# One TensorE side group per head instead of two in a chunked recurrence, with eight level products packed into two banks

## The chip, the cores and the metric

The kernel runs on one core of one Trainium2 chip. The time is that of the device, in microseconds, for one execution of the whole program; the lower, the better. TensorE is written PE in the profile, its weight loads PEld, VectorE DVE, ScalarE ACT, GpSimd POOL and SyncE, which issues most of the DMAs, SP.

## What is computed

The reference is two model blocks on 512 tokens of width 2048, in float32. The first block normalises the input, multiplies it by a large `w_in`, and splits the product into a gated short convolution and a recurrent part; the second is an attention and retention block. Nearly all of the arithmetic is in dense products with weight matrices. What the change touches is the recurrent part, cut to its core here (8 heads, 128 features in each, log decays `log_f` that differ by feature):

```python
def step(state, inp):                      # one chunk of tokens, all heads
    qn, kn, vn, fn = inp
    b = jnp.cumsum(fn, axis=2)
    inter = jnp.einsum('bhtk,bhkv->bhtv', qn * jnp.exp(b), state)
    diff = b[:, :, :, None, :] - b[:, :, None, :, :]
    decay = jnp.exp(jnp.where(causal, diff, 0.0)) * causal_f
    a = jnp.einsum('bhtk,bhtsk,bhsk->bhts', qn, decay, kn)
    o = inter + jnp.einsum('bhts,bhsv->bhtv', a, vn)
    b_last = b[:, :, -1:, :]
    state = (jnp.exp(b_last[:, :, 0, :])[..., None] * state
             + jnp.einsum('bhsk,bhsv->bhkv', kn * jnp.exp(b_last - b), vn))
    return state, o
```

The matrix `a` has the decay inside its sum over the features, so it is no plain product of q and k.

## The kernel before

**Dense work.** Each weight matrix is read in units of 256 rows by 512 columns (`UNITS`), by SP into `RAW`. ScalarE rounds a unit to its high part (`WH`, line 395), VectorE subtracts to get the low part (`WL`, line 418), and TensorE makes three products for each (high by high, high by low, low by high) into four banks of PSUM, in `pe_dense` at line 366. A group of 512 columns takes 16 steps of k for a 2048-row matrix, 12 dense matmuls in each. `hi_upto` and `lo_upto` let the splits run two units ahead of TensorE.

**Side work.** Each engine's program is a generator. After each dense step, `Turns.after_step` lets one piece of the queue `specials` be written, up to its next bare `yield`, and one of `chores`. The recurrence of the eight heads is such side work: `hgrn_pe`, `hgrn_act`, `hgrn_dve`, `hgrn_sp`, one after the other, among the dense groups `cg`, `xa`, `bg`, `za` of each half (heads 0 to 3 in the first, 4 to 7 in the second). So the order is fixed when the program is written, and `idle(n)` leaves n steps without a side piece.

**One head.** The kernel computes `a` for chunks of 128 tokens by levels. Level 0 is the diagonal; level L pairs blocks of h = 2^(L-1) tokens with the block behind them, so that the decay can be put into q and k one level at a time. For each level ScalarE makes two exponentials (lines 895, 901), VectorE multiplies them into q and k (lines 1000 and 1004; the rows are those of `level_rows`), and then brings two running sums on (lines 1008, 1012). Levels 2 to 7 have only four rows of scratch, `XX[:, 0..2]` and `XX4`, and levels 5 and 6 use rows of levels 3 and 2 again: hence in `hgrn_dve`, for `lev > 4`, a wait for the products of levels 0 to 3.

TensorE makes all products of a head in tiles of 32 output rows (`tile_position=(0, y)`), in two side groups:

- the first, after `idle(3)`: levels 0 and 1 (line 782, 16 matmuls) into one bank, levels 2 and 3 (line 798, 32 matmuls) into the other;
- the second, four steps later: levels 4 and 5 (line 798, 32 matmuls), levels 6 and 7 (line 782, 8 and 8 matmuls).

Each of these float32 matmuls is two passes in the trace, so a group is 96 passes. Two of the eight banks (6 and 7) are for side work, and all side groups take them in turn. VectorE copies the products out of the banks into `AT` by `take_diagonal` (line 937), `take_pairs` (948), `take_within` (958) and `take_across` (974). After the two groups come the sums over a chunk (line 825, 6 passes) and the values (lines 857 and 860, 14 passes), both in whole 128-row form.

Of the kernel before, what the change touches and what calls it, by code (L numbers as in the profile page):

```python
# [224 lines left out]
def build(nc, xT, pT, vec, logits, cst, masks, ident, w_in, w_a, w_b, w_o, w_gate, w_proj,  # L225
# [528 lines left out]
    XX4 = sb("XX4", [512], F32, W0 + 98560)  # L754
    XQ = sb("XQ", [16, 48], F32, W0 + 98560)

    def level_rows(lev):
        return XX4[:, :] if lev == 7 else XX[:, {2: 2, 3: 1, 4: 0, 5: 1, 6: 2}[lev]]

    QUERIES = XX[:, 1]  # L760
# [6 lines left out]
    def hgrn_pe(i, hh):  # L767
        half = hh // 4
        kk, q = KK[:, i], Q[:, i]

        def product_bank(levels):
            b, was = special_bank(("prod", hh, levels[0]), dve, ("take", hh, levels[-1]))
            for lev in levels:
                banks["prod", hh, lev] = banks["prod", hh, levels[0]]
            if was:
                T.wait_ge(was[0], (yield was))
            return b

# [12 lines left out]
        def within_tiles(lev, b, at):  # L791
            h = 1 << (lev - 1)
            T.wait_ge(dve, (yield dve, ("xl", hh, lev)))
            for n in range(16):
                y = 32 * n % 128
                t = level_rows(lev)[:, 32 * n:32 * n + 32]
# [5 lines left out]
        def across_tiles(b):  # L802
            T.wait_ge(dve, (yield dve, ("xl", hh, 6)))
            x = level_rows(6)
            for n in range(8):
                c, p = n // 2, n % 2
                tile_product(b, 64 * p + 32 * (c % 2), 32 * (c // 2),
                             x[:, 64 * n:64 * n + 32], x[:, 64 * n + 32:64 * n + 64])

        def across_halves(b):  # L810
            T.wait_ge(dve, (yield dve, ("xl", hh, 7)))
            x = level_rows(7)
            for n in range(8):
                c, p = n // 2, n % 2
                ins = tile_product(b, 64 * (c % 2) + 32 * p, 64 + 64 * (c // 2),
                                   x[:, 64 * n - 32 * p:64 * n - 32 * p + 32], x[:, 128 * c + 64:128 * c + 128])
            return ins

        def chunk_sums(b):
            for j in range(4):  # L820
                T.wait_ge(ev_a, (yield ev_a, (("iv", half), j)))
            T.wait_ge(keys_turned, (yield keys_turned, hh))
            T.wait_ge(keys_turned2, (yield keys_turned2, hh))
            for c in range(3):
                ins = nc.tensor.matmul(b[:, CH[c]], KT[:, c], VN[:, c, 128 * i:128 * i + 128], start=True, stop=True)  # L825
            ins.then_inc(side.sem, side.step(("sums", hh)))

        yield from idle(3)
        b = yield from product_bank((0, 1))
        yield from pairs_and_diagonal(b)  # L830
        b = yield from product_bank((2, 3))
        yield from within_tiles(2, b, 0)
        ins = yield from within_tiles(3, b, 256)
        ins.then_inc(side.sem, side.step(("prod", hh, 3)))
        yield
        yield from idle(3)
        b = yield from product_bank((4, 5))
        yield from within_tiles(4, b, 0)
        yield from within_tiles(5, b, 256)
        b = yield from product_bank((6, 7))  # L840
# [80 lines left out]
    def hgrn_dve(i, hh):  # L921
        half = hh // 4
        lf, kk, q, r = LF[:, i], KK[:, i], Q[:, i], RR[:, :]

        def take_diagonal():
            b = bank[banks["prod", hh, 0]]
# [12 lines left out]

        def take_pairs():  # L940
            b = bank[banks["prod", hh, 0]]
            V.wait_ge(side, (yield side, ("prod", hh, 3)))
# [7 lines left out]

        def take_within(lev):
            h = 1 << (lev - 1)
            at = 256 if lev in (3, 5) else 0
            src = bank[banks["prod", hh, lev]][:, at:at + 256].rearrange("p (c n x) -> p c n x", c=4, x=h)
            msk = late(MASK[:, lev], lev).unsqueeze(1).broadcast_to([128, 4, 64 // h, h])
            V.wait_ge(side, (yield side, ("prod", hh, 3 if lev < 4 else 7)))
            V.wait_ge(dve, (yield dve, ("take", hh, lev - 1)))
            nc.vector.copy_predicated(ATD.rearrange("p c (n x) -> p c n x", x=2 * h)[:, :, :, h:], msk, src
                                      ).then_inc(dve.sem, dve.step(("take", hh, lev)))

        def take_across(lev):
            b = bank[banks["prod", hh, lev]]
            V.wait_ge(side, (yield side, ("prod", hh, 7)))
            V.wait_ge(dve, (yield dve, ("take", hh, lev - 1)))
            w = 32 * (lev - 5)
            for odd in range(2):
                for p in range(2):
                    if lev == 6:
                        y, rows, cols, at = 64 * p + 32 * odd, slice(64 * p, 64 * p + 32), 64 * p + 32, 0
                    else:  # L970
                        y, rows, cols, at = 64 * odd + 32 * p, slice(32 * p, 32 * p + 32), 64, 64
                    src = b[y:y + 32, at:at + 2 * w].rearrange("p (c t) -> p c t", c=2)
                    dst = ATD[rows, odd::2, cols:cols + w]
                    ins = nc.vector.tensor_copy(dst, src)
            ins.then_inc(dve.sem, dve.step(("take", hh, lev)))

        for lev in range(1, 8):
# [7 lines left out]
            V.wait_ge(act, (yield act, ("up", hh, lev)))  # L985
            V.wait_ge(ev_d, (yield ev_d, (("q", half), i)))
            if lev > 4:
                V.wait_ge(side, (yield side, ("prod", hh, 3)))
            elif hh % 4:
                V.wait_ge(dve, (yield dve, ("o", hh - 1)))  # L990
            if lev == 1:
# [4 lines left out]
                                        E[:, 1:512:2].rearrange("p (n x) -> p n x", x=16), ALU.mult  # L996
                                        ).then_inc(dve.sem, dve.step(("xu", hh, 1), ("xl", hh, 1)))
            else:
                X = level_rows(lev)
# [6 lines left out]
            if lev > 1:  # L1006
# [22 lines left out]
        if hh:  # L1029
# [5 lines left out]
        yield from take_within(4)  # L1035
        yield from take_within(5)
# [5 lines left out]
        yield from take_across(6)  # L1042
        yield
        yield from take_across(7)
        yield
        yield
# [1727 lines left out]
```

## Time and profile before

| | us |
|---|---|
| median of 3 runs | 2510.53 (2509.77 to 2511.0) |
| profiled execution | 2509.97 |
| its span, first to last instruction | 2508.7 |
| PE busy | 2502.2 (100%) |
| PEld busy | 2075.9 (83%) |
| DVE busy | 1358.9 (54%) |
| ACT busy | 918.4 (37%) |
| POOL busy | 149.5 (6%) |

The span is what the trace covers; the execution has 1.3 us around it. Busy time of PE is the union of its matmuls' modelled durations, which overlap: a dense matmul is shown as 0.39 us long, while the next one starts 0.23 us behind it. So the distance between starts, not the duration, is what a matmul costs. In a timeline row "x32" are instructions merged into one row, the first number is when the first of them starts, the second how long they last together, to the modelled end of the last.

### The profile page before, as it was taken

What the parts mean: (1) busy time and instruction counts of PE and PEld (TensorE: products, weight loads), DVE (VectorE), ACT (ScalarE), POOL (GpSimd) and SP (SyncE); (2) the same over time, 40 slices, a digit from 0 to 9 for tenths busy, and PEclk for the clock granted to TensorE, in tenths of its full rate; (3) what the DMA queues carried; (4) which work ended last, traced back from release to release, by engine and by line L of the source; (5) the groups of instructions that cost most, each with busy time, mean ns of one, the idle gap of its engine ahead of it and who ended that gap; (6) DMA issues with size and microseconds to landing.
All of it is one profiled execution on the core that took longest, in us unless ns stands there. A gap on an engine that the chain in (4) does not pass through costs nothing.

```text
span 2508.7 us, 31305 instructions
## 1 busy us (share of the span) xinstructions
PE 2502.2 (100%) x12614; PEld 2075.9 (83%) x12614; DVE 1358.9 (54%) x2248; ACT 918.4 (37%) x1259; POOL 149.5 (6%) x195
## 2 busy tenths in 40 slices
PE   9999999999999999999999999999999999999999
PEld 8888888888888888888888888888888888888888
DVE  7557744567544555655443363485256555665425
ACT  6633325333332222322232253443344344544423
POOL 0011110012100000000001103200000000000001
PEclk9999999999999999999999999999999999999999
DMA  5333333333335666666443232236222243433432
GB/s 192 110 96 95 96 105 95 95 95 100 100 93 164 213 218 214 218 212 212 149 161 110 93 101 93 93 101 178 92 76 76 85 125 101 113 106 112 178 101 101
DMA packets 213633, 317.95 MB, mean 127 GB/s; under 512 B 66736, under 2 KB 69680, under 8 KB 212464
## 3 DMA queue, kind: packets, MB, share of 16 engines
q1 hardware_dynamic: 208592, 312.55, 40.2%
q0 software_dynamic: 4320, 2.99, 0.5%
q8 instruction: 99, 1.62, 0.3%
q10 hardware_dynamic: 576, 0.42, 0.1%
q14 instruction: 46, 0.38, 0.1%
HBM read 295.43 MB, written 8.39 MB: 121 GB/s over the span
## 4 chain that ended last, share of the span: by engine, by line
PE 100%; ACT 0%; DVE 0%; issue 0%; ACTq 0%; DVEq 0%
PE bank L366 94%; PE bank L1449 1%; PE bank L1450 1%; PE bank L1451 1%; PE bank L798 0%; PE bank L857 0%; PE bank L782 0%; PE bank L860 0%; PE bank L825 0%; PE bank L1841 0%; PE bank L1955 0%; PE bank L1953 0%; PE bank L1954 0%; PE bank L467 0%; ACT OT L2266 0%; PE bank L472 0%
## 5 line engine op out<-in xcount | busy, mean ns | idle before, releaser
L366 PE MATMUL bank<-XH,WH 128*128 128x512 f32 (+1 forms) x2776 | 1078.7, 390 | 0.0
L366 PE MATMUL bank<-XH,WL 128*128 128x512 f32 (+1 forms) x2776 | 1074.5, 389 | 0.0
L366 PE MATMUL bank<-XL,WH 128*128 128x512 f32 (+1 forms) x2776 | 1074.0, 389 | 0.0
L418 DVE TENSOR_TENSOR WL<-RAW,WH 128x1024 fp32r<-128x1024 f32 x430 | 530.1, 1234 | 760.6 <-ACT WH L395 760.0
L395 ACT CAST WH<-RAW 128x1024 fp32r<-128x1024 f32 x430 | 450.1, 1048 | 1113.4 <-PE bank L366 1102.2
L366 PEld LDWEIGHTS bank<-XH,WL 128*128 128x128 f32 x2776 | 521.0, 188 | 108.1 <-DVE WL L418 0.2
L366 PEld LDWEIGHTS bank<-XH,WH 128*128 128x128 f32 x2776 | 521.0, 188 | 107.7 <-ACT WH L395 0.2
L366 PEld LDWEIGHTS bank<-XL,WH 128*128 128x128 f32 x2776 | 521.2, 188 | 107.1 <-issue 0.5
L366 PE MATMUL bank<-WH,XL 128*128 128x512 f32 x384 | 149.4, 389 | 0.0
L366 PE MATMUL bank<-WH,XH 128*128 128x512 f32 x384 | 149.4, 389 | 0.0
L366 PE MATMUL bank<-WL,XH 128*128 128x512 f32 x384 | 149.4, 389 | 0.0
L1234 DVE CUSTOM_DVE_ANT_0 AST<-AST,CB 128x512 f32<-128x512 f32 x192 | 125.1, 685 | 10.0 <-DMA AST<-in_w_ada 9.8
L366 PE MATMUL bank<-YH,WH 128*128 128x512 f32 x256 | 97.7, 389 | 0.0
L366 PE MATMUL bank<-YH,WL 128*128 128x512 f32 x256 | 97.6, 389 | 0.0
L366 PE MATMUL bank<-YL,WH 128*128 128x512 f32 x256 | 97.6, 389 | 0.0
L366 PEld LDWEIGHTS bank<-WH,XH 128*128 128x128 f32 x384 | 72.1, 188 | 15.1
L366 PEld LDWEIGHTS bank<-WL,XH 128*128 128x128 f32 x384 | 72.1, 188 | 14.9
L366 PEld LDWEIGHTS bank<-WH,XL 128*128 128x128 f32 x384 | 72.1, 188 | 14.9
L2597 POOL TENSOR_TENSOR AC<-AC,GT 128x512 f32<-128x512 f32 x15 | 22.7, 1512 | 748.0 <-ACT GT L2087 746.4
L366 PEld LDWEIGHTS bank<-YL,WH 128*128 128x128 f32 x256 | 48.0, 188 | 10.0
L366 PEld LDWEIGHTS bank<-YH,WL 128*128 128x128 f32 x256 | 48.0, 188 | 10.0
L366 PEld LDWEIGHTS bank<-YH,WH 128*128 128x128 f32 x256 | 48.1, 188 | 10.0
(351 smaller groups left out, 1882.7 us busy)
## 6 DMA issues: line engine op xcount, KB each, us to landing
RAW<-in_w_in SPq DMA_DIRECT2D x303, 512.0 KB, 3.8
AST<-in_w_ada SPq DMA_DIRECT2D x192, 256.0 KB, 4.1
RAW<-in_w_o SPq DMA_DIRECT2D x32, 512.0 KB, 3.7
RAW<-in_w_gate SPq DMA_DIRECT2D x32, 512.0 KB, 3.6
RAW<-in_w_out SPq DMA_DIRECT2D x32, 512.0 KB, 3.7
RAW<-in_w_a SPq DMA_DIRECT2D x16, 512.0 KB, 4.2
RAW<-in_w_b SPq DMA_DIRECT2D x16, 512.0 KB, 4.3
PT<-ZT SPq DMA_DIRECT2D x256, 32.0 KB, 1.9
```

Of the source, the lines that this page charges most:

```text
L366: ins = nc.tensor.matmul(bank[b][:, cols], l, r[:, cols], start=first, stop=final)
L395: nc.scalar.copy(high_of(m), RAW[:, m % NRAW]).then_inc(hi.sem, hi.step(m))
L418: nc.vector.tensor_tensor(low_of(m), RAW[:, m % NRAW], high_of(m).bitcast(F32), ALU.subtract).then_inc(lo.sem, lo.step(m))
L1234: nc.vector.tensor_tensor_reduce(AST[:, n % 3], AST[:, n % 3], CB[:, q % 2], 1.0, 0.0, ALU.mult, ALU.add, PART[:, n:n + 1]).then_inc(dve.s ...
L1449: nc.tensor.matmul(b, high, right_high, start=start, stop=False)
L1450: nc.tensor.matmul(b, high, right_low, start=False, stop=False)
L1451: return nc.tensor.matmul(b, low, right_high, start=False, stop=stop)
L2597: nc.gpsimd.tensor_tensor(AC[:, 0], AC[:, 0], GT[:, j % 4], ALU.add).then_inc(pool.sem, pool.step(("acc1", j)))
```

## The change

`JOINED = range(8)` names the heads that have one side group instead of two; it is all of them. What it does for a head:

- `level_rows` gives levels 5, 6 and 7 rows of their own, in buffers that are idle at that time: rows of `YA` for heads 0 to 3, of `O` for head 4, of `LF`, `KK` and `Q` for heads 5 to 7. The wait at `lev > 4` goes.
- `hgrn_pe` has `idle(7)` and then all eight levels at once, at the step where the second group was. Levels 0 to 3 go to one bank and 4 to 7 to the other. To fit, levels 3 and 5 are packed by the new `half_of_tiles`: 64 columns instead of 256. The number of matmuls stays.
- `hgrn_dve` takes no product at levels 5 and 6 any more. All takes stand behind the last level. Levels 3 and 5 are taken by the new `take_half_of_tiles`, in four pieces each instead of one.
- The event that tells VectorE of levels 0 to 3 is now that of level 7 (`early`).

```diff
-    def level_rows(lev):
+    JOINED = range(8)
+
+    def level_rows(hh, lev):
+        if hh in JOINED and lev > 4:
+            if hh < 4:
+                return YA[:, lev - 1]
+            return O[:, lev] if hh == 4 else (LF, KK, Q)[lev - 5][:, hh - 5]
         return XX4[:, :] if lev == 7 else XX[:, {2: 2, 3: 1, 4: 0, 5: 1, 6: 2}[lev]]
...
+        def half_of_tiles(lev, b, at):
+            h = 1 << (lev - 1)
+            T.wait_ge(dve, (yield dve, ("xl", hh, lev)))
+            for n in range(16):
+                y = 32 * (n % 4)
+                t = level_rows(hh, lev)[:, 32 * n:32 * n + 32]
+                c = slice(at + 16 * (n // 4), at + 16 * (n // 4) + 16)
+                nc.tensor.matmul(b[y:y + 32, c].rearrange("p (n x) -> p n x", x=h), t,
+                                 late(t, lev), start=True, stop=True, tile_position=(0, y))
...
-        yield from idle(3)
-        b = yield from product_bank((0, 1))
-        yield from pairs_and_diagonal(b)
-        b = yield from product_bank((2, 3))
-        yield from within_tiles(2, b, 0)
-        ins = yield from within_tiles(3, b, 256)
-        ins.then_inc(side.sem, side.step(("prod", hh, 3)))
-        yield
-        yield from idle(3)
-        b = yield from product_bank((4, 5))
-        yield from within_tiles(4, b, 0)
-        yield from within_tiles(5, b, 256)
-        b = yield from product_bank((6, 7))
-        yield from across_tiles(b)
-        ins = yield from across_halves(b)
+        if hh in JOINED:
+            yield from idle(7)
+            b = yield from product_bank((0, 1, 2, 3))
+            yield from pairs_and_diagonal(b)
+            yield from within_tiles(2, b, 192)
+            yield from half_of_tiles(3, b, 448)
+            b = yield from product_bank((4, 5, 6, 7))
+            yield from within_tiles(4, b, 0)
+            yield from half_of_tiles(5, b, 256)
+            yield from across_tiles(b, 320)
+            ins = yield from across_halves(b, 384)
...
+        def take_half_of_tiles(lev):
...
+            for y in range(0, 128, 32):
+                rows = slice(y, y + 32)
+                if lev == 5:
+                    ins = nc.vector.tensor_copy(ATD[y:y + 16, :, y + 16:y + 32],
+                                                b[y:y + 16, at:at + 64].rearrange("p (c x) -> p c x", c=4))
+                    continue
+                src = b[rows, at:at + 64].rearrange("p (c n x) -> p c n x", c=4, x=h)
+                msk = late(MASK[rows, lev, rows], lev).unsqueeze(1).broadcast_to([32, 4, 16 // h, h])
+                ins = nc.vector.copy_predicated(
+                    ATD[rows, :, rows].rearrange("p c (n x) -> p c n x", x=2 * h)[:, :, :, h:], msk, src)
...
             if lev > 4:
-                V.wait_ge(side, (yield side, ("prod", hh, 3)))
+                if hh not in JOINED:
+                    V.wait_ge(side, (yield side, ("prod", hh, 3)))
...
-            if lev == 5:
+            if lev == 5 and hh not in JOINED:
                 yield from take_diagonal()
                 yield from take_pairs()
-            if lev == 6:
+            if lev == 6 and hh not in JOINED:
                 yield from take_within(2)
                 yield from take_within(3)
...
+        if hh in JOINED:
+            yield from take_half_of_tiles(3)
+            yield from take_within(4)
+            yield
+            yield from take_half_of_tiles(5)
+            yield from take_across(6)
+            yield
+            yield from take_across(7)
+            yield
```

TensorE, the products of head 0, before; `XQ` and `XX` hold the levels' rows, and 48 dense matmuls (left out at "...") stand between the groups:

```order
L366 MATMUL bank<-XH,WL 128x512
L782 MATMUL bank<-XQ,KK 32x48 x16
L798 MATMUL bank<-XX 32x16 x32
L366 MATMUL bank<-XH,WH 128x512
...
L366 MATMUL bank<-XH,WL 128x512
L798 MATMUL bank<-XX 32x16 x32
L782 MATMUL bank<-XX 32x32 x8
L782 MATMUL bank<-XX_89 32x64 x8
L366 MATMUL bank<-XH,WH 128x512
```

And the same place in the changed kernel, where line 788 is the old 782, line 804 the old 798, and line 815 the new `half_of_tiles`:

```order
L366 MATMUL bank<-XH,WL 128x512
L788 MATMUL bank<-XQ,KK 32x48 x16
L804 MATMUL bank<-XX 32x16 x16
L815 MATMUL bank<-XX 32x16 x16
L804 MATMUL bank<-XX 32x16 x16
L815 MATMUL bank<-YA 32x16 x16
L788 MATMUL bank<-YA 32x32 x8
L788 MATMUL bank<-YA 32x64 x8
L366 MATMUL bank<-XH,WH 128x512
```

The 96 matmuls of a head are the same ones; 48 of them moved 48 dense matmuls down, to stand ahead of the other 48.

VectorE, head 0, before, from the last products of level 6 to the last take; `WL` is a dense split:

```order
L1012 TENSOR_TENSOR LF<-LF 128x8x32
L958 COPY_PREDICATED AT<-MASK,bank 128x128x2
L958 COPY_PREDICATED AT<-MASK,bank 128x64x4
...
L418 TENSOR_TENSOR WL<-RAW,WH 128x1024
L1027 TENSOR_TENSOR KEYS<-KK,EE 128x384
L1032 STREAM_TRANSPOSE ZK<-KEYS 128x384
L958 COPY_PREDICATED AT<-MASK,bank 128x32x8
L958 COPY_PREDICATED AT<-MASK,bank 128x16x16
L418 TENSOR_TENSOR WL<-RAW,WH 128x1024
L1040 TENSOR_TENSOR XX<-Q,EE 128x384
L974 COPY AT<-bank 32x2x32 x4
L974 COPY AT<-bank 32x2x64 x4
```

In the changed kernel from the same split on (line 1076 is the old 1027, 1081 the old 1032, 966 the old 937, 977 the old 948, 987 the old 958, 1022 the old 974; 999 and 1004 are the new takes of levels 5 and 3):

```order
L1076 TENSOR_TENSOR KEYS<-KK,EE 128x384
L1081 STREAM_TRANSPOSE ZK<-KEYS 128x384
L966 COPY_PREDICATED AT<-MASK,bank 32x4x32 x4
L977 COPY_PREDICATED AT<-MASK,bank 32x4x16 x4
L987 COPY_PREDICATED AT<-MASK,bank 128x128x2
L418 TENSOR_TENSOR WL<-RAW,WH 128x1024
L1094 TENSOR_TENSOR XX<-Q,EE 128x384
L1004 COPY_PREDICATED AT<-MASK,bank 32x4x4x4 x4
L987 COPY_PREDICATED AT<-MASK,bank 128x32x8
L999 COPY AT<-bank 16x4x16 x4
L1022 COPY AT<-bank 32x2x32 x4
L418 TENSOR_TENSOR WL<-RAW,WH 128x1024
```

The takes of levels 0 to 3 have left the levels' own steps and stand behind the keys; the splits keep their number and their order among the steps.

## Rows read from the trace of the kernel before

**Rows 1.** The page: TensorE's busy time, its instruction queue, the chain that ended last.
```profile
PE 2502.2 (100%) x12614; PEld 2075.9 (83%) x12614; DVE 1358.9 (54%) x2248; ACT 918.4 (37%) x1259; POOL 149.5 (6%) x195
...
q8 instruction: 99, 1.62, 0.3%
...
PE 100%; ACT 0%; DVE 0%; issue 0%; ACTq 0%; DVEq 0%
```

**Rows 2.** Timeline of PE (start, duration, instruction, count): first group of head 0.
```profile
148.06 0.39 PE L366 MATMUL bank<-XH,WL 128*128 128x512 f32 x1
148.37 0.55 PE L782 MATMUL bank<-XQ,KK 128*32 128x48 f32 x32
148.74 0.73 PE L798 MATMUL bank<-XX 128*32 128x16 f32 x64
149.40 0.50 PE L366 MATMUL bank<-XH,WH 128*128 128x512 f32 x1
149.74 0.39 PE L366 MATMUL bank<-XL,WH 128*128 128x512 f32 x1
...
152.04 0.39 PE L366 MATMUL bank<-XH,WL 128*128 128x512 f32 x1
```

**Rows 3.** Timeline of PE: second group of head 0, the dense matmuls around it.
```profile
160.20 0.39 PE L366 MATMUL bank<-XH,WL 128*128 128x512 f32 x1
160.52 0.70 PE L798 MATMUL bank<-XX 128*32 128x16 f32 x62
...
161.56 0.50 PE L366 MATMUL bank<-XH,WH 128*128 128x512 f32 x1
161.90 0.39 PE L366 MATMUL bank<-XL,WH 128*128 128x512 f32 x1
```

**Rows 4.** Timeline of PE: the 128-row sums of head 0.
```profile
172.36 0.39 PE L366 MATMUL bank<-XH,WL 128*128 128x512 f32 x1
...
173.48 0.40 PE L366 MATMUL bank<-XL,WH 128*128 128x512 f32 x1
```

**Rows 5.** Waits of PEld (line, releaser, us in total, times, longest).
```profile
PEld bank L782 <- issue: 2.8, 8, 0.4
PEld bank L798 <- issue: 2.1, 6, 0.4
...
PEld bank L366 <- DVE WL L418: 0.2, 1, 0.2
```

**Rows 6.** DMA queues (packets, MB, share of 16 engines), 210 to 215 us.
```profile
q8 instruction: 1, 0.02, 1.6%
```

**Rows 7.** Timeline of PE: start of the second group of head 2.
```profile
262.75 0.71 PE L798 MATMUL bank<-XX 128*32 128x16 f32 x62
```

**Rows 8.** Timeline of DVE: around that group.
```profile
255.39 1.23 DVE L948 COPY_PREDICATED AT<-MASK,bank 32x64 f32<-32x64 uint16 x4
...
260.04 1.21 DVE L958 COPY_PREDICATED AT<-MASK,bank 128x256 f32<-128x256 uint16 x2
...
261.49 0.42 DVE L1004 TENSOR_TENSOR XX<-KK,EE 128x256 f32<-128x256 f32 x1
...
266.95 0.90 DVE L958 COPY_PREDICATED AT<-MASK,bank 128x256 f32<-128x256 uint16 x2
...
269.35 2.13 DVE L974 COPY AT<-bank 32x64 f32<-32x64 f32 x8
```

**Rows 9.** Groups of DVE instructions by form (count, busy us, mean ns, idle before).
```profile
L948 DVE COPY_PREDICATED AT<-MASK,bank 32x64 f32<-32x64 uint16 x32 | 9.5, 298 | 0.6
L974 DVE COPY AT<-bank 32x64 f32<-32x64 f32 x32 | 7.0, 218 | 0.3
```

**Rows 10.** Windows (busy us by engine, then granted clock, DMA share, GB/s).
```profile
160.00:162.00 2.00, 2.00 (x101) 1.51 (x100) 1.97 (x4) 1.73 (x3) 0.53 (x1) 1.00 0.05 4
...
2502.00:2505.00 3.00, 1.57 (x15) 1.33 (x13) 2.47 (x9) 2.15 (x7) 0.00 (x0) 1.00 1.01 384
2505.00:2508.70 3.70, 0.00 (x0) 0.00 (x0) 0.39 (x1) 0.45 (x1) 0.00 (x0) 0.77 0.77 293
```

More of the change, by code:

```diff
@@ L800, in within_tiles, with across_tiles, across_halves @@
             return ins
-        def across_tiles(b):
+        def half_of_tiles(lev, b, at):
[3 more added lines that the diff above has]
+                y = 32 * (n % 4)
+                t = level_rows(hh, lev)[:, 32 * n:32 * n + 32]
+                c = slice(at + 16 * (n // 4), at + 16 * (n // 4) + 16)
+                nc.tensor.matmul(b[y:y + 32, c].rearrange("p (n x) -> p n x", x=h), t,
+                                 late(t, lev), start=True, stop=True, tile_position=(0, y))
+        def across_tiles(b, at):
             T.wait_ge(dve, (yield dve, ("xl", hh, 6)))
-            x = level_rows(6)
+            x = level_rows(hh, 6)
             for n in range(8):
                 c, p = n // 2, n % 2
-                tile_product(b, 64 * p + 32 * (c % 2), 32 * (c // 2),
+                tile_product(b, 64 * p + 32 * (c % 2), at + 32 * (c // 2),
                              x[:, 64 * n:64 * n + 32], x[:, 64 * n + 32:64 * n + 64])
-        def across_halves(b):
+        def across_halves(b, at):
             T.wait_ge(dve, (yield dve, ("xl", hh, 7)))
-            x = level_rows(7)
+            x = level_rows(hh, 7)
             for n in range(8):
                 c, p = n // 2, n % 2
-                ins = tile_product(b, 64 * (c % 2) + 32 * p, 64 + 64 * (c // 2),
+                ins = tile_product(b, 64 * (c % 2) + 32 * p, at + 64 * (c // 2),
                                    x[:, 64 * n - 32 * p:64 * n - 32 * p + 32], x[:, 128 * c + 64:128 * c + 128])
@@ L826, in chunk_sums @@
             ins.then_inc(side.sem, side.step(("sums", hh)))
-        yield from idle(3)
-        b = yield from product_bank((0, 1))
-        yield from pairs_and_diagonal(b)
-        b = yield from product_bank((2, 3))
-        yield from within_tiles(2, b, 0)
-        ins = yield from within_tiles(3, b, 256)
-        ins.then_inc(side.sem, side.step(("prod", hh, 3)))
-        yield
-        yield from idle(3)
-        b = yield from product_bank((4, 5))
-        yield from within_tiles(4, b, 0)
-        yield from within_tiles(5, b, 256)
-        b = yield from product_bank((6, 7))
-        yield from across_tiles(b)
-        ins = yield from across_halves(b)
+        if hh in JOINED:
[9 more added lines that the diff above has]
+            ins = yield from across_halves(b, 384)
+        else:
+            yield from idle(3)
+            b = yield from product_bank((0, 1))
+            yield from pairs_and_diagonal(b)
+            b = yield from product_bank((2, 3))
+            yield from within_tiles(2, b, 0)
+            ins = yield from within_tiles(3, b, 256)
+            ins.then_inc(side.sem, side.step(("prod", hh, 3)))
+            yield
+            yield from idle(3)
+            b = yield from product_bank((4, 5))
+            yield from within_tiles(4, b, 0)
+            yield from within_tiles(5, b, 256)
+            b = yield from product_bank((6, 7))
+            yield from across_tiles(b, 0)
+            ins = yield from across_halves(b, 64)
         ins.then_inc(side.sem, side.step(("prod", hh, 7)))
@@ L923, in hgrn_dve @@
         lf, kk, q, r = LF[:, i], KK[:, i], Q[:, i], RR[:, :]
+        early = ("prod", hh, 7 if hh in JOINED else 3)
         def take_diagonal():
@@ L931, in take_diagonal @@
                 V.wait_ge(pool, (yield pool, "at0"))
-            V.wait_ge(side, (yield side, ("prod", hh, 3)))
+            V.wait_ge(side, (yield side, early))
             for y in range(0, 128, 32):
@@ L941, in take_pairs @@
             b = bank[banks["prod", hh, 0]]
-            V.wait_ge(side, (yield side, ("prod", hh, 3)))
+            V.wait_ge(side, (yield side, early))
             V.wait_ge(dve, (yield dve, ("take", hh, 0)))
@@ L952, in take_within @@
             h = 1 << (lev - 1)
-            at = 256 if lev in (3, 5) else 0
+            at = 256 if lev in (3, 5) else 192 if lev == 2 and hh in JOINED else 0
             src = bank[banks["prod", hh, lev]][:, at:at + 256].rearrange("p (c n x) -> p c n x", c=4, x=h)
             msk = late(MASK[:, lev], lev).unsqueeze(1).broadcast_to([128, 4, 64 // h, h])
-            V.wait_ge(side, (yield side, ("prod", hh, 3 if lev < 4 else 7)))
+            V.wait_ge(side, (yield side, early if lev < 4 else ("prod", hh, 7)))
             V.wait_ge(dve, (yield dve, ("take", hh, lev - 1)))
@@ L959, in take_within @@
                                       ).then_inc(dve.sem, dve.step(("take", hh, lev)))
+        def take_half_of_tiles(lev):
+            h = 1 << (lev - 1)
+            at = 448 if lev == 3 else 256
+            b = bank[banks["prod", hh, lev]]
+            V.wait_ge(side, (yield side, ("prod", hh, 7)))
+            V.wait_ge(dve, (yield dve, ("take", hh, lev - 1)))
+            for y in range(0, 128, 32):
[8 more added lines that the diff above has]
+                    ATD[rows, :, rows].rearrange("p c (n x) -> p c n x", x=2 * h)[:, :, :, h:], msk, src)
+            ins.then_inc(dve.sem, dve.step(("take", hh, lev)))
         def take_across(lev):
+            a6, a7 = (320, 384) if hh in JOINED else (0, 64)
             b = bank[banks["prod", hh, lev]]
@@ L968, in take_across @@
                     if lev == 6:
-                        y, rows, cols, at = 64 * p + 32 * odd, slice(64 * p, 64 * p + 32), 64 * p + 32, 0
+                        y, rows, cols, at = 64 * p + 32 * odd, slice(64 * p, 64 * p + 32), 64 * p + 32, a6
                     else:
-                        y, rows, cols, at = 64 * odd + 32 * p, slice(32 * p, 32 * p + 32), 64, 64
+                        y, rows, cols, at = 64 * odd + 32 * p, slice(32 * p, 32 * p + 32), 64, a7
                     src = b[y:y + 32, at:at + 2 * w].rearrange("p (c t) -> p c t", c=2)
@@ L998, in hgrn_dve @@
             else:
-                X = level_rows(lev)
+                X = level_rows(hh, lev)
                 nc.vector.tensor_tensor(vw(X)[:, :, h:], vw(q)[:, :, h:], vw(E)[:, :, h:], ALU.mult
@@ L1034, in hgrn_dve @@
         yield
-        yield from take_within(4)
-        yield from take_within(5)
+        if hh in JOINED:
+            yield from take_diagonal()
+            yield from take_pairs()
+            yield from take_within(2)
+        else:
+            yield from take_within(4)
+            yield from take_within(5)
         yield
@@ L1041, in hgrn_dve @@
                                 ).then_inc(dve.sem, dve.step(("queries", hh)))
[L1042 to L1046, printed above, removed]
+        if hh in JOINED:
+            yield from take_half_of_tiles(3)
+            yield from take_within(4)
+            yield
[3 more added lines that the diff above has]
+            yield from take_across(7)
+            yield
+        else:
+            yield from take_across(6)
+            yield
+            yield from take_across(7)
+            yield
+            yield
         V.wait_ge(side, (yield side, ("sums", hh)))
```

2 lines of the change are left out of this document (removed).

## The prediction

> **What bounds the kernel now.** I read the page first. TensorE is busy for 2502.2 of 2508.7 us, and the chain of what ended last is TensorE by 100% [rows 1]. So the time is the sum of the distances between TensorE's starts, and another engine counts only where it makes TensorE wait. The list of TensorE's waits shows none of that in the recurrent part: the one wait for a low part of weights in the whole program is 0.2 us, and what stands ahead of the side groups is "issue", 0.35 us each (2.8 us over 8 times), a cost of going over and not a wait for data [rows 5]. The view that decides is therefore the timeline of TensorE around the side groups.
>
> **What a group costs now.** Dense matmuls start every 0.2267 us: from 152.04 to 160.20 there are 36 steps, 8.16 us [rows 2, 3]. Around the first group of head 0 the last dense one starts at 148.06 and the twelfth one behind the group at 152.04 [rows 2]. Undisturbed, twelve steps are 12 x 0.2267 = 2.72 us; they took 3.98. The group costs 1.26 us. The same over two steps of the second group: 161.90 - 160.20 = 1.70, less 0.45, is 1.25; with the 0.02 to 0.03 us by which the next dense ones are a little slow (the first group has 1.68 - 0.45 = 1.23 over two steps, and 1.26 over twelve), 1.27.
>
> How much of that is the 96 passes, and how much is paid once for a group? The last pass starts 0.73 - 0.18 = 0.55 us behind 148.74 (a pass of this form is shown as 0.18 us long), at 149.29. So the passes themselves go from 148.37 to 149.29, 0.92 us, 9.6 ns each. The rest, 1.26 - 0.92 = 0.34 us, comes once: the first pass starts 0.31 us behind the last dense matmul instead of 0.23; the first dense one 0.11 us behind the last pass; the next one 0.34 us behind that instead of 0.23; and the slow steps after it. In the second group the same reading gives about 0.90 us of passes and 0.35 to 0.37 once.
>
> **The change, part by part.**
>
> *One group instead of two.* No matmul goes and none is added; 192 passes stand in one row, 0.92 + 0.90 us and one distance between them of 0.01. Once per head 0.34 us falls away. The distance between a 48-column pass and a 16-column one is already inside the first group, as that from 16 to 32 columns is in the second, and neither shows. Eight heads: 8 x 0.34 = 2.7 us. The bounds: no more can go than all that is paid once, 8 x 0.37 = 3.0 us. For the lower end I take the sums, six passes that keep the 128-row form: 173.48 - 172.36 = 1.12, less 0.45, is 0.67 us [rows 4], so that at a ninth to a tenth of a microsecond for each pass (128 of 512 columns would be a quarter of 0.2267, two passes and the weight loads make it more) hardly 0.1 us is paid once. If only that were saved, it is 0.8 us. The groups here change from 128 to 32 rows and back, and their own rows have the 0.34, so I take 2.7.
>
> *Packing of levels 3 and 5.* 16 matmuls of 16 columns each as before, at other columns of the bank. Four matmuls in a row go to four different sets of 32 rows, as in line 782 now, whose 48 columns cost 11.6 ns a pass (148.37 to 148.74 for 32) against 8.7 for 16 columns [rows 2]. Cost nothing; at worst 11.6 - 8.7 = 3 ns for 64 passes of 8 heads, 1.5 us, which I don't expect since the width does not change.
>
> *Waits on TensorE.* The merged group needs the rows of level 7. For head 2, which has the convolution beside it and is the tightest that I saw, VectorE finishes them at 261.49 + 0.42 = 261.91 [rows 8], and the second group starts at 262.75 [rows 7]. Now this group comes 1.26 us sooner, because the first one no longer stands ahead of it: it would need them at 261.5 and wait 0.4 us. But the takes of levels 0 to 3 leave VectorE's steps ahead of level 7: lines 937 and 948 with about 1.23 us each and line 958 with 1.21 [rows 8], 3.7 us. Even if ScalarE's exponentials give back half of that, the rows are there some 1.5 to 3 us early. Cost nothing; if this cover were missing, 8 x 0.4 = 3.2 us, just the gain.
>
> *The takes behind the group.* VectorE now has all takes between the group and the values. Those of levels 0, 1 and 2 are 3.1 us, level 3 becomes four pieces of 298 ns where it was one of 0.6, level 5 four of at most 218 ns where it was one of 0.45 [rows 8, 9]; 1.0 us more for a head, 8 us in all, on an engine that is busy for 54%. The sums take the bank of levels 0 to 3 again, four dense steps behind the group, some 10.9 us; takes 0 to 3 with a split (1.2) and the queries (0.55) are 3.1 + 1.2 + 0.55 + 1.2 = 6.1 us. Before the values stand six dense steps and the sums, 17 us; all takes with two splits are about 11 us. Behind these takes on VectorE stand the splits for the dense work, and TensorE would wait for them. They run two units ahead, 24 dense matmuls or 5.4 us for each, and so two or three more microseconds of delay are taken up. Cost nothing, below nothing neither: no TensorE wait is there to be won. The banks go in turn as before, with the wait of the sums for take 3 instead of take 5.
>
> *The sum.* The profiled execution, 2509.97 us (span 2508.7), becomes 2507.3. The median of the runs is 0.56 us above it, 2510.53; by the same difference it becomes **2507.8 us**, 0.11% less. A measurement of this kernel can tell about 0.2%, 5 us, from no change.
>
> **Rivals.**
>
> *A. The supply of instructions.* TensorE's instructions come by queue q8 in 99 packets, 1.62 MB for 25,228 matmuls and weight loads [rows 1, 6]: 64 bytes each, 256 in a packet. In the window of 5 us around the second group of head 1 one packet takes 1.6% of 16 engines, 1.28 us [rows 6]. In dense work a packet lasts 29 us. A group of now is 192 instructions, less than one packet; the merged one is 384 in 1.83 us, so that 256 are used up in 1.2 us. If only the packet in use and the next one are held, then in about half of the heads ((384 - 256)/256) a whole packet falls inside the group, and the one behind it is asked for too late, by 0.5 to 1.2 us. Four heads at 0.8 us are 3.2 us: 2510.53 - 2.7 + 3.2 = 2511.0. For it: no group of now is long enough to show the limit. Against it: nothing in the trace says how many packets are held, and the pace within the groups does not fall towards their end.
> The Trainium skill ("TensorE: Matmul & The Clock Gate", Architectural detail) gives TensorE a queue of 64 instructions, and in the same page (Wait — 56ns, not 53.3ns?) some 62 ns of sequencer for a matmul when decoding in hardware is off. By that a group would run fast only while the queue lasts, and 96 passes would take about 4 us; the rows have 1.26, so this rule does not hold here, and by the rows the pace is the same for the second half of a merged group.
>
> *B. The clock falls (slower).* TensorE's granted clock is 1.00 in the window of a group, and of the whole run only the last window, in which TensorE does nothing, has less, 0.77 [rows 10]. If a group of twice the length let it fall to its lower level, 1.2 instead of 2.4 GHz, for about 4 us around each, half of these are lost: 8 x 2 = 16 us, or 2510.53 - 2.7 + 16 = 2523.8. It decides from four such spells on (8 - 2.7 = 5.3 us). Against it: in a merged group TensorE does per microsecond just what it does in a group of now, and weights are loaded in it without a break.
> The Trainium skill (same page, What's actually happening) says that the clock is set by how busy TensorE was of late; by it this rival is possible, and no row here shows it outside of idleness.
>
> *C. The takes crowd VectorE after all.* With the convolution beside heads 2 and 6, a split comes late once a head by 1 us: +2 for two heads, 2509.8; if for all eight, 2515.8.
>
> *D. Nothing moves.* The once-paid part is bound to the form of the passes and comes back inside the long group: 2510.5.
>
> **Chances.** Forecast 0.72; A 0.12; B 0.03; C 0.05; D 0.08. The forecast's own spread is 2506.8 to 2509.7 (its bounds of 0.8 to 3.0 us, and 0.7 us for the measurement); A and D add the upper end. Range 2506.4 to 2511.2. Since no more than 3.0 us is to be had, faster by over 0.2% needs something that I have not seen: 0.03. Slower by over 0.2% is B and the worst of C: 0.04. Within 0.2%: 0.93.
>
> **What the profile after would show.** Eight side groups of 192 passes, each 2.2 us over the dense pace, and no group where the first one was; the wait "issue" ahead of side groups of 32 rows 8 times instead of 14 to 16; the takes of levels 0 to 3 behind the group, VectorE idle for a moment ahead of them; the same dense pace and clock. For A: a hole inside some of the groups and not in others, with a packet of q8 beside it. For B: a granted clock below 1.00 behind the groups. For C: TensorE waiting for `WL` between 130 and 700 us. The forecast is wrong if the eight groups cost more than 2.3 us each, or if any dense stretch got a hole.

## The result, and the profile after

| | median of the runs (range) | runs | span of the profiled execution |
|---|---|---|---|
| before | 2510.53 us (2509.77 to 2511.02) | 5 | 2508.7 us |
| after | 2524.49 us (2523.58 to 2527.45) | 5 | 2523.2 us |

The changed kernel is slower: ratio 1.0058, with a 95% interval of 1.0046 to 1.007. The forecast was 2507.8 us with a range up to 2511.2, so it was wrong in sign as well as in size.

The page after, in the lines that answer to [rows 1]:

```profile
PE 2507.0 (99%) x12614; PEld 2081.3 (82%) x12614; DVE 1366.2 (54%) x2296; ACT 918.2 (36%) x1259; POOL 149.5 (6%) x195
...
q8 instruction: 99, 1.62, 0.3%
...
PE 99%; issue 0%; ACT 0%; DVE 0%; ACTq 0%; DVEq 0%
```

The counts on TensorE and the 99 instruction packets are the same. The chain is still TensorE's, but its busy time is now 16.2 us short of the span (2523.2 - 2507.0), where it was 6.5 us short before. The waits of the weight loads (line, releaser, us in total, times, longest), which answer to [rows 5], show what has come in:

```profile
PEld bank L788 <- issue: 8.0, 9, 3.6
PEld bank L815 <- issue: 4.7, 2, 2.5
...
PEld bank L366 <- DVE WL L418: 0.2, 1, 0.2
```

The longest "issue" was 0.4 us before and is 3.6 us now. The wait for `WL` is the same single 0.2 us, and it lies in the first 100 us. In the recurrent part one side group's wait is put down to VectorE, but with 0.35 us it is as long as that of the other groups, which is put down to "issue": VectorE costs TensorE nothing there. The timeline of TensorE (start, duration, instruction, count, in brackets the idle time ahead of the first of them) for head 0, which answers to [rows 3]:

```profile
159.01 0.39 PE L366 MATMUL bank<-XH,WL 128*128 128x512 f32 x1
159.32 0.55 PE L788 MATMUL bank<-XQ,KK 128*32 128x48 f32 x32
...
160.64 0.58 PE L815 MATMUL bank<-YA 128*32 128x16 f32 x26
163.35 0.21 PE L815 MATMUL bank<-YA 128*32 128x16 f32 x2 [2.12 <-issue]
...
163.42 0.54 PE L788 MATMUL bank<-YA 128*32 128x32 f32 x29
163.89 0.50 PE L366 MATMUL bank<-XH,WH 128*128 128x512 f32 x1
164.22 0.40 PE L366 MATMUL bank<-XL,WH 128*128 128x512 f32 x1
...
164.76 0.63 PE L366 MATMUL bank<-XH,WH 128*128 128x512 f32 x1
165.19 0.63 PE L366 MATMUL bank<-XL,WH 128*128 128x512 f32 x1
...
167.32 0.63 PE L366 MATMUL bank<-XH,WH 128*128 128x512 f32 x1
167.75 0.52 PE L366 MATMUL bank<-XL,WH 128*128 128x512 f32 x1
168.10 0.40 PE L366 MATMUL bank<-XH,WL 128*128 128x512 f32 x1
```

Two things are new here. First, the group stops in the middle of one instruction form: between passes 28 and 29 of the 32 of level 5's products TensorE does nothing for 2.12 us. I call such a gap a hole, and measure it below from start to start (here 2.31 us). The rows `YA` of that product are not the reason: VectorE wrote its last rows, those of level 7, at 155.79 to 156.21, three microseconds before the group began. Second, from 164.76 on the dense matmuls start 0.43 us apart instead of 0.2267 and last 0.63 us instead of 0.39. The windows (busy us by engine, granted clock, DMA share, GB/s) for heads 0, 6 and 7 at and behind their holes, and for head 3 inside its hole and behind it:

```profile
164.60:168.00 3.40, 3.40 (x10) 2.61 (x9) 3.26 (x9) 0.00 (x0) 0.00 (x0) 0.50 0.07 11
...
594.70:601.50 6.80, 5.60 (x14) 4.32 (x15) 5.07 (x14) 0.00 (x0) 2.19 (x5) 0.50 0.14 24
...
652.70:656.10 3.40, 3.40 (x9) 2.65 (x8) 3.25 (x11) 0.00 (x0) 0.00 (x0) 0.50 0.14 23
...
317.80:319.70 1.90, 0.16 (x12) 0.00 (x0) 0.00 (x0) 0.00 (x0) 1.69 (x4) 1.00 0.20 37
...
319.80:323.20 3.40, 3.40 (x24) 2.75 (x24) 2.89 (x9) 0.02 (x1) 1.58 (x3) 1.00 0.21 38
```

The granted clock is 0.50, its level of 1.2 GHz, where it was 1.00 around the groups in [rows 10]. TensorE had stood still just before; in head 6 it still stood when the clock fell, at 594.7 us, and went on at 595.9. Behind head 3's hole, the shortest of the four, the clock stayed at 2.4 GHz.

The holes have a packet of instructions beside them. For head 0, the DMA queues in 160.9 to 163.4 us (packets, MB, share of 16 engines); the 4.9 us ahead of that window have none:

```profile
q8 instruction: 1, 0.02, 2.4%
```

2.4% of 16 engines in 2.5 us is 0.96 us for this packet. By its own record it is under way from 161.06 to 162.01, and work goes on at 163.35.

Head 2 has no hole. This is its group, in the same view, with its neighbours:

```profile
264.90 0.39 PE L366 MATMUL bank<-XH,WL 128*128 128x512 f32 x1
265.22 0.55 PE L788 MATMUL bank<-XQ,KK 128*32 128x48 f32 x32
...
266.66 0.56 PE L788 MATMUL bank<-YA 128*32 128x32 f32 x31
267.15 0.50 PE L366 MATMUL bank<-XH,WH 128*128 128x512 f32 x1
267.49 0.39 PE L366 MATMUL bank<-XL,WH 128*128 128x512 f32 x1
```

267.49 - 264.90 = 2.59, less 0.45 for two dense steps, is 2.14 us (2.16 over twelve steps). That is what the prediction had for all eight.

Why head 2 and not head 0? I counted TensorE's instructions (weight loads, matmuls, and its own waits) in order of start, and took the number modulo 256, since [rows 1] gives 256 instructions to a packet:

| head | group starts at | hole, start to start | after minus before, over the head |
|---|---|---|---|
| 0 | 135 | 2.31 us | +3.87 us |
| 1 | 204 | | -0.21 |
| 2 | 16 | | -0.38 |
| 3 | 84 | 2.00 | +1.81 |
| 4 | 187 | | -0.07 |
| 5 | 255 | | -0.23 |
| 6 | 67 | 3.66 | +5.84 |
| 7 | 135 | 2.57 | +3.80 |

The heads sum to +14.43 us; with 0.07 us at the program's start that is the whole difference of the spans, 14.5. All four holes are at the same place: the first instruction behind each is number 193 modulo 256, counted from 0. The holes are 10.5 us; 26 dense steps at the lower clock, 0.20 us too long each, are 5.2 (with those that are partly slow 5.8, 1.6 behind head 0's hole, 2.6 at head 6's and 1.6 behind head 7's); what is left, about 2 us less, is the groups that are one instead of two.

### The profile page after: what moved, and what is told of

It is laid out like the page before. It is cut to its first block, busy times and chain, and to the rows that moved or that the text cites. A ratio compares the mean times of both kernels' runs of the same rounds, so it can differ in the third digit from the quotient of the medians.

```text
span 2523.2 us, 31353 instructions
## 1 busy us (share of the span) xinstructions
PE 2507.0 (99%) x12614; PEld 2081.3 (82%) x12614; DVE 1366.2 (54%) x2296; ACT 918.2 (36%) x1259; POOL 149.5 (6%) x195
## 4 chain that ended last, share of the span: by engine, by line
PE 99%; issue 0%; ACT 0%; DVE 0%; ACTq 0%; DVEq 0%
PE bank L366 94%; PE bank L1513 1%; PE bank L1515 1%; PE bank L1514 1%; PE bank L788 0%; PE bank L885 0%; PE bank L888 0%; PE bank L841 0%; PE bank L815 0%; PE bank L804 0%; PE bank L1905 0%; PE bank L2019 0%; PE bank L2018 0%; PE bank L2017 0%; PE bank L467 0%
```

## The experiments

The theory from here on: TensorE gets its instructions in packets of 256; a packet is asked for at a fixed place of the count, and a long row of quick instructions reaches the end of what is held before the next packet has come. Rivals: the hole belongs to the data or the banks of the heads 0, 3, 6 and 7; to the packed form of levels 3 and 5; to the number of instructions whatever their place; and for the clock, that it is the long group and not the hole that lets it fall. The kernel before had a median of 2510.27 us beside the first four experiments and 2510.47 beside the others.

**shift128: the same work, 128 instructions later in the count.**

```diff
         for n in range(11):
             nc.tensor.matmul(bank[7][:, 0:128], ONES, ONES, start=True, stop=True)
+        for n in range(32):
+            y = 32 * (n % 4)
+            nc.tensor.matmul(bank[7][y:y + 32, 0:16], ONES[:, 0:32], ONES[:, 0:16], start=True, stop=True,
+                             tile_position=(0, y))
```

> The changed kernel with 32 tiny matmuls (128 instructions) more at the very start, which moves every side group by 128 instructions in TensorE's stream. Supply theory: the holes sit where the stream's index is 193 modulo 256 and the packet behind it was asked for at or just before the group's start. With the shift the groups of heads 0, 3, 6 and 7 start at 7, 212, 195 and 7 modulo 256 and lose their holes; those of heads 1 (76), 5 (127) and 2 (144) get one of 2 to 3.7 us, head 4 (59) a small one near its end. Total 2520 to 2527 us. Rival, the long group itself or a semaphore in it makes the hole: the holes stay in heads 0, 3, 6, 7 and the time is that of the changed kernel plus about 1 us.

Measured: 2523.77 us (2521.9 to 2525.36; four runs), ratio 1.0053 (1.0039 to 1.0067). Heads 0, 3, 6 and 7 have no hole any more. Holes are now in head 1 (1.89 us), head 2 (3.64), head 5 (2.34), and just behind the group of head 4, in the dense matmuls (2.43). All four are at 193 modulo 256 again. Head 4's is larger than the small one that was expected. TensorE's timeline: head 0, now clean; head 2, now with a hole; the dense matmuls behind head 4:

```profile
160.13 0.39 PE L366 MATMUL bank<-XH,WL 128*128 128x512 f32 x1
160.45 0.55 PE L788 MATMUL bank<-XQ,KK 128*32 128x48 f32 x32
...
162.71 0.50 PE L366 MATMUL bank<-XH,WH 128*128 128x512 f32 x1
163.04 0.39 PE L366 MATMUL bank<-XL,WH 128*128 128x512 f32 x1
...
265.52 0.37 PE L815 MATMUL bank<-YA 128*32 128x16 f32 x22
269.35 0.26 PE L815 MATMUL bank<-YA 128*32 128x16 f32 x5 [3.46 <-issue]
...
494.76 0.39 PE L366 MATMUL bank<-XH,WL 128*128 128x512 f32 x1
497.20 0.80 PE L366 MATMUL bank<-XH,WH 128*128 128x512 f32 x1 [2.05 <-issue]
```

So the place in the count decides and not the head, its buffers or its banks: 128 instructions at the program's start, over 100 us earlier, moved every hole. Even a dense matmul can stand behind such a hole; it was only the next one in the row. The window from 269 to 275 us, behind head 2's hole, has the clock at 0.50.

**packed_two: packing, rows and late takes, but two groups.**

```diff
-            yield from idle(7)
+            yield from idle(3)
...
             yield from half_of_tiles(3, b, 448)
+            yield
+            yield from idle(3)
             b = yield from product_bank((4, 5, 6, 7))
```

> The changed kernel's packing, own rows and late takes, but TensorE's products in two groups again at their old steps. Supply theory: 192 instructions in a group, no hole, 2510.5 us within 1. If packing, rows or the late takes cost anything, over 2512.

Measured: 2510.24 us (2510.07 to 2510.71), ratio 1.0 (0.999 to 1.0009); each head within about 0.01 us of before, no hole. The longest wait at a side group is 0.4 us, as before, whatever it is put down to (16 groups in all, one of them in a row that is not shown):

```profile
PEld bank L788 <- issue: 2.8, 8, 0.4
PEld bank L804 <- DVE KEYS L1078: 1.4, 4, 0.4
...
PEld bank L804 <- issue: 1.1, 3, 0.4
```

All parts of the change other than the joining cost nothing.

**join1245 and join0367: the change for four heads each.**

```diff
-    JOINED = range(8)
+    JOINED = (1, 2, 4, 5)
```

and `(0, 3, 6, 7)` in the other.

> Only heads 1, 2, 4 and 5 have one group; the alignment of the stream is that of the changed kernel, in which these four had no hole. Supply theory: no hole, no fall of the clock, 0.6 to 1.4 us less than the kernel before: 2509.1 to 2509.9. Rival (merging as such costs): half of the changed kernel's loss, about 2517.

> Only heads 0, 3, 6 and 7 have one group. Supply theory: four holes of 2 to 3.7 us and two or three falls of the clock, the whole loss of the changed kernel and a little more: 2523 to 2527. Rival: half of the loss, about 2517.

Measured: join1245 2509.29 us (2508.92 to 2510.37), ratio 0.9996 (0.9987 to 1.0004), heads -0.25, -0.34, -0.05 and -0.25 us, no hole. join0367 2523.74 us (2522.21 to 2525.72), ratio 1.0053 (1.004 to 1.0067), four holes of 2.56, 2.37, 2.97 and 2.39 us at 193 modulo 256, and the clock fell behind all four: 30 slow steps, 6.0 us. Its heads cost 4.12, 3.76, 4.19 and 3.65 us. The window of join1245 over the whole recurrent part, and the waits of join0367:

```profile
130.00:700.00 570.00, 570.00 (x4045) 473.15 (x4044) 342.26 (x687) 203.28 (x320) 73.39 (x135) 1.00 0.35 98
```

```profile
PEld bank L788 <- issue: 8.1, 10, 2.9
PEld bank L815 <- issue: 4.8, 2, 2.5
```

In the first TensorE is busy for 570.00 of 570.00 us at a clock of 1.00. The loss is wholly in the four heads that were expected to have it; the other four give 0.9 us together, which is no difference that the interval can tell. How often the clock falls differs between executions of one kernel: over the whole run the granted clock was 0.997 in the profiled execution of join0367 and 0.998 or 0.999 in its three others, which were 1.9 to 3.5 us shorter. So the counts of falls here are those of the profiled executions.

**near_two: two groups again, with one dense step between them.**

```diff
-            yield from idle(7)
+            yield from idle(6)
...
             yield from half_of_tiles(3, b, 448)
+            yield
             b = yield from product_bank((4, 5, 6, 7))
```

> The changed kernel with one dense step (12 matmuls, 2.7 us) between levels 0 to 3 and 4 to 7. Supply theory: a request has 2.7 us more until the next packet is needed; with 3.5 to 5 us for a request, holes of at most 1 to 2 us are left in heads 0, 3, 6 and 7, at 193 modulo 256, no fall of the clock, and the once-paid 0.34 us is back: 2510.5 to 2514. Rival, the number of side instructions within some microseconds decides: the loss stays at 10 us or more.

Measured: 2510.82 us (2510.01 to 2511.63), ratio 1.0001 (0.9991 to 1.001). No hole in any head, not even the small ones that the expectation allowed. Head 0, its two groups:

```profile
157.18 0.39 PE L366 MATMUL bank<-XH,WL 128*128 128x512 f32 x1
157.50 0.55 PE L788 MATMUL bank<-XQ,KK 128*32 128x48 f32 x32
...
158.52 0.50 PE L366 MATMUL bank<-XH,WH 128*128 128x512 f32 x1
...
161.17 0.39 PE L366 MATMUL bank<-XH,WL 128*128 128x512 f32 x1
161.49 0.44 PE L804 MATMUL bank<-XX 128*32 128x16 f32 x32
...
162.53 0.50 PE L366 MATMUL bank<-XH,WH 128*128 128x512 f32 x1
```

The 24 instructions of a dense step are more instructions, not fewer, but they take 2.7 us, and that is enough for a packet. So what counts is the time in which 256 instructions are used up.

**hole_only: a stall without a long group.** TensorE of the kernel before is made to wait behind its first side group for a take of VectorE.

```diff
         ins.then_inc(side.sem, side.step(("prod", hh, 3)))
+        T.wait_ge(dve, (yield dve, ("take", hh, 0)))
         yield
```

> The kernel before, with TensorE made to wait behind each head's first group until VectorE has taken the diagonal; a stall of 2 to 4 us in each of eight heads, with no long group anywhere. Clock theory: the granted clock falls to its lower level behind stalls of over about 2.2 us, whatever made them, and dense starts are then 0.43 us apart; 24 us of stalls and 5 to 15 us of slow clock: 2540 to 2550. Rival, the clock falls because of the long run of small tiles: no fall, about 2534.

Measured: 2552.02 us (2551.57 to 2552.46; two runs), ratio 1.0166 (1.0147 to 1.0184), 2 us above what was expected. The stalls were 3.3 us in four heads and 3.8 to 3.9 us in the others, and the clock fell at all eight, in four of them while TensorE still stood: 64 slow steps, 12.8 us. TensorE's timeline and the windows of head 1's:

```profile
206.81 0.53 PE L798 MATMUL bank<-XX 128*32 128x16 f32 x39
210.43 0.67 PE L366 MATMUL bank<-XH,WH 128*128 128x512 f32 x1 [3.08 <-DVE AT L938]
210.90 0.63 PE L366 MATMUL bank<-XL,WH 128*128 128x512 f32 x1
```

```profile
210.60:214.00 3.40, 3.40 (x9) 2.64 (x10) 0.98 (x4) 0.00 (x0) 0.00 (x0) 0.50 0.06 24
...
214.00:218.00 4.00, 4.00 (x19) 3.29 (x18) 1.44 (x4) 1.67 (x3) 0.00 (x0) 1.00 0.00 0
```

The clock falls behind a stall made by a wait as well, with groups of the old length. That a long group is needed for the fall, as the rival has it, is out.

**hole_short: the same with a shorter stall**, for the rows of level 5:

```diff
         ins.then_inc(side.sem, side.step(("prod", hh, 3)))
+        T.wait_ge(dve, (yield dve, ("xl", hh, 5)))
         yield
```

> The same with a shorter wait, for the rows of level 5: stalls of 1 to 2 us in eight heads. Clock theory: no fall of the clock, 8 to 16 us of stalls alone: 2519 to 2527. If the clock falls here too, the length of a stall is not what decides.

Measured: 2524.04 us (2522.59 to 2525.5; two runs), ratio 1.0054 (1.0036 to 1.0073). The stalls are 1.90 to 1.95 us in the even heads and 1.34 or 1.35 us in the odd ones. My expectation of no fall held for the odd heads and for heads 2 and 4; behind those of head 0 (1.90) and head 6 (1.95) the clock fell, 14 slow steps or 2.8 us. Windows of head 0 (the stall, then behind it) and behind head 1's stall:

```profile
149.40:151.70 2.30, 0.58 (x22) 0.44 (x11) 1.75 (x6) 1.00 (x3) 0.00 (x0) 1.00 0.79 230
...
151.70:155.10 3.40, 3.40 (x10) 2.62 (x9) 3.25 (x10) 0.72 (x2) 0.00 (x0) 0.50 0.02 6
...
205.20:209.00 3.80, 3.76 (x17) 3.11 (x18) 3.02 (x10) 0.66 (x1) 0.00 (x0) 1.00 0.47 138
```

Near 2 us the length of the stall alone doesn't decide: two of four with the same length fell. What else does, these runs don't tell.

**delayed6: six heads joined, at chosen places of the count.** Heads 0, 3 and 6 begin their recurrence two steps later, so that the joined groups stand at 183, 252, 180, 187, 255 and 183 modulo 256. Heads 2 and 6 keep two groups, since their joined ones would stand near 64 and 115 (worked out from the distances between the groups in the changed kernel).

```diff
-    JOINED = range(8)
+    JOINED = (0, 1, 3, 4, 5, 7)
+    DELAY = {0: 2, 3: 2, 6: 2}
...
+        yield from idle(DELAY.get(hh, 0))
```

(the last line at the head's start in `hgrn_pe`, `hgrn_act`, `hgrn_dve` and `hgrn_sp`)

> Heads 0, 1, 3, 4, 5 and 7 have one group, and heads 0, 3 and 6 start two steps later on every engine, which puts the merged groups at 183, 252, 180, 187, 255 and 183 modulo 256, behind the request at about 142. Supply theory: no hole and no fall of the clock; six times 0.2 to 0.34 us less than the kernel before: 2508.4 to 2509.3. If a merged group still has a hole, the rule of the place in the stream is wrong.

Measured: 2509.84 us (2508.87 to 2510.59), ratio 0.9997 (0.9989 to 1.0006). No hole, and the clock is 1.00 throughout the recurrent part:

```profile
130.00:700.00 570.00, 570.00 (x4045) 473.65 (x4045) 343.09 (x699) 201.56 (x319) 73.08 (x135) 1.00 0.35 98
```

Heads 0, 3 and 7, which lost 3.87, 1.81 and 3.80 us when joined at 135, 84 and 135, lose nothing at 183, 180 and 183. Here the theory said beforehand at which places a joined group is free. (Heads 1, 4 and 5 had been free already, at 204, 187 and 255.) The time is 0.5 to 1.4 us above what I expected of it. The recurrent part of its profile is 1.10 us shorter than before's, but that execution reached it 1.04 us later; the profiles of all these kernels reach it 0.06 to 1.04 us later than before's, and the median can't be split that finely. It is no difference from before that can be told, and neither is join1245.

## Why the prediction was wrong, point by point

*What bounds the kernel.* Right: TensorE's starts alone make the time, before and after. One reading was not: in the list behind [rows 5] two of the 16 side groups are put down to VectorE (`PEld bank L798 <- DVE LF L1012: 0.7, 2, 0.4`), so it does show waits on data there. They are 0.35 us each like the other fourteen, and nothing hung on them.

*One group instead of two, 0.34 us a head.* Held in head 2 (2.14 to 2.16 us a group, forecast 2.2). The other clean groups cost 2.31 to 2.47 us, since small gaps of 80 to 145 ns stand inside them. Two groups cost 2 x 1.27 = 2.54, so the gain is 0.07 to 0.38 us a head, about 2 us over eight (an estimate; the four of join1245 gave 0.9) instead of 2.7. The cause of these small gaps was not tried.

*Packing, waits, takes: nothing.* Right, by packed_two (ratio 1.0) and by the single 0.2 us wait for `WL`. In head 0 VectorE even stood idle before its takes, 2.3 us of it for the hole; in head 2, with the convolution beside it, it did not, and the first take (267.57 us) began 0.4 us after the next dense matmul (267.15). VectorE's timeline at head 0, changed kernel:

```profile
164.06 1.22 DVE L966 COPY_PREDICATED AT<-MASK,bank 32x128 f32<-32x128 uint16 x4 [4.84 <-issue]
```

*Rival A, 0.8 us a hole, chance 0.12.* This is the step that failed: the forecast's sum puts the supply of instructions at nothing, and where A prices it, at 3.2 us, it is far too low; measured are 10.5 us of holes and 5.8 us of slow clock behind them. A's mechanism was right, down to the sign that would show it (a hole in some groups, a packet of q8 beside it). That it was half of the heads is partly luck: A wanted a whole packet inside the group, while the runs have the hole where the group begins between 59 and 144 of the count. Its price was wrong twice:

- *The hole itself.* I worked from the time that a packet is under way, 1.28 us [rows 6], against the 1.2 us in which 256 instructions go. The packets beside the four holes took 0.92 to 1.41 us, quite as expected, but the time until TensorE goes on is much longer. In the dense stretches of the kernel before no packet starts earlier than number 151 of the count modulo 256; the place at which it is asked for must be a little ahead of that, and 142 is my estimate. It is needed at 193 of the next 256, 307 instructions later. In a joined group the instructions from 142 to the hole take about 1.5 us, and TensorE resumes 3.5 to 5 us after 142 has gone. Part of that is ahead of the packet; 1.3 to 1.5 us come behind its end (162.01 to 163.35 at head 0). So a hole is 2.0 to 3.7 us, not 0.5 to 1.2. What sets the spread between 3.5 and 5 us I have not tried. By the same estimate the 307 instructions ahead of each of the twelve holes of all runs went in 1.4 to 2.4 us, and where there was no hole they never took less than 4.3 us (near_two, four heads); nothing was run in between.
- *What a hole sets off.* I had A and B as two separate cases: A without the clock, and B, the clock, from the length of the group alone, with the remark that TensorE does just as much per microsecond as before. But a hole is exactly a stretch in which it does nothing, and at three of the four the clock went to 1.2 GHz, 5.8 us more. B's price, 2523.8, came near the measured 2524.49 by accident. The 4 us of slow clock that it gives each group came from no row, and its mechanism, the long group, is refuted by hole_only, where the clock fell behind groups of the old length, and by join1245, where it stayed.

Together, for the profiled executions: 2509.97 + 10.5 + 5.8 - 1.8 is 2524.5, as measured; the 1.8 is what is left over, so this sum is no check of it. Had I taken A's holes and asked what an idle TensorE does to the clock, [rows 10] had the hint: the only window below 1.00 was the one in which TensorE did nothing. The chance of A was too small as well. "Nothing in the trace says how many packets are held" was an unknown cost for which only one end, up to 3.2 us, went into the range, and the argument against it ("the pace within the groups does not fall towards their end") could not bear on it: a group of 192 instructions is over long before the 307 are used up.

The Trainium skill ("Advanced Engine Details and Errata", ISA Cache) bears on that point: it has lines of 16 KB, 256 instructions, and only two of them. The Trainium skill ("Runtime: NRT & Kernel Launch", Instruction fetch mechanics) has the same two lines, adds that TensorE has 128 KiB or 2048 instructions, and calls the crossing of a boundary "mostly hidden". The traces fit two lines: the twelve holes of the changed kernel, shift128 and join0367 come within 384 quick instructions or, in one case (shift128, head 4), just behind them, which 2048 held ones would have covered. The Trainium skill ("TensorE: Matmul & The Clock Gate", Architectural detail) gives TensorE a queue of 64. If the sequencer runs ahead of execution by that much, a block would be freed at 193 - 64 and the next one needed 256 + 64 = 320 instructions later; this is an estimate from the page's figure, near the 307 that I estimate from the packets, and that reading is argued, not shown. Where the page of the Trainium skill has "mostly hidden", the holes of 1.9 to 3.7 us decide otherwise for rows of short matmuls.

## What to carry to other kernels

Count the instructions of a burst and not only its time: here up to 192 of TensorE's in a row (0.9 us) were free everywhere, 384 (1.8 us) were free at some places of the program and cost 2 to 6 us at others, and one dense step of 2.7 us between the halves made them free again. Measured over the 307 instructions from the estimated place of the request to the need, 4.3 us and more were enough and 2.4 us and less were not. A change that adds 128 instructions far ahead can move such holes, so a time that jumps by 3 us without a reason in the data calls for the instruction queue's packets beside the gap. And price every hole in TensorE together with the clock behind it: a stall can bring the fall of the clock with it, as ten of the twelve holes did.

## What the runs showed of the hardware that I had not expected

- TensorE's holes from supply are at one place of the count, 193 modulo 256, in 12 of 12 cases (changed kernel, shift128, join0367). A joined group of 384 had one inside where it started at 67, 76, 84, 127, 135 or 144 of that count, and one just behind it at 59; at 7, 16, 180 to 212, 252 and 255 it had none.
- From the place of the request, as estimated, to TensorE's next instruction are 3.4 to 5.6 us over the twelve holes, though the packet itself is under way for 0.9 to 1.4 us; 1.3 to 1.5 us of the time come behind its end.
- At stalls of 3.3 to 3.9 us made by a wait the granted clock fell in 8 of 8 cases (hole_only), behind 1.90 to 1.95 us in 2 of 4, behind 1.34 or 1.35 us in 0 of 4 (hole_short). Of the twelve holes those of 2.31 us and more had it, those of 1.89 and 2.00 us did not. A fall cost 1.4 to 3 us beside the stall.
